# Feed-forward up product as seven block products, with the block sums spread over VectorE and GpSimd

## What is computed

```
h = layer_norm(DN_ALPHA * x + m, ln1_g[i], ln1_b[i])
f = jnp.square(jax.nn.relu(h @ mlp_w1[i])) @ mlp_w2[i]
e = jax.nn.sigmoid(h @ ple_w_gate[i]) * (p[i] @ ple_w_proj[i])
x = layer_norm(DN_ALPHA * h + f + e, ln2_g[i], ln2_b[i])
```

```
mod = jax.nn.silu(c.astype(F32)) @ w_ada + b_ada
```

## Time and profile before

| | us |
|---|---|
| median of 3 runs | 2377.9 |
| lowest and highest | 2377.06, 2378.38 |
| span of the profiled execution | 2375.1 |
| around the span, up to the median | 2.8 |

### The profile page before, as it was taken

How to read it: one execution, slowest core, us unless ns; L and a number is a source line. 1 busy time by engine, 2 the same in 40 slices (tenths; PEclk the granted TensorE clock), 3 DMA queues, 4 the chain that set the end, 5 groups by cost and what they waited for, 6 DMA issues and landing times.

```text
span 2375.1 us, 30964 instructions
## 1 busy us (share of the span) xinstructions
PE 2250.5 (95%) x13454; PEld 1516.2 (64%) x13454; DVE 737.4 (31%) x1301; ACT 411.4 (17%) x845; POOL 523.9 (22%) x451
## 2 busy tenths in 40 slices
PE   9999999999999999999988888899999998888887
PEld 8776676686668899888333333378998863333333
DVE  5533224524216755523100000055753221000001
ACT  3320112620103331211000000033112020000001
POOL 2387622257752045000000000012530000000000
PEclk9999999999999999999999999999999999999999
DMA  7377732358751442349999999953332799999998
GB/s 278 109 309 285 304 133 86 129 193 339 303 217 65 138 143 90 107 168 400 425 428 428 428 428 428 416 212 114 121 136 97 283 409 427 427 428 428 428 427 317
DMA packets 136850, 654.76 MB, mean 276 GB/s; under 512 B 9864, under 2 KB 15112, under 8 KB 108168
## 3 DMA queue, kind: packets, MB, share of 16 engines
q1 hardware_dynamic: 136712, 652.72, 69.0%
HBM read 651.64 MB, written 1.05 MB: 275 GB/s over the span
## 4 chain that ended last, share of the span: by engine, by line
PE 73%; DMA 21%; DVE 3%; ACT 1%; issue 1%; SPq 0%; POOL 0%; DVEq 0%; ACTq 0%
PE bank L798 72%; DMA ring<-in_w_exp_up 11%; DMA PRGT<-in_w_exp_up 5%; DMA PRGT<-in_w_exp_down 3%; DMA PRGT<-in_w_exp_gate 1%; ACT R L3378 1%; PE bank L1428 0%; DVE sm L2174 0%; POOL PRGT L3476 0%; SPq L712 0%; DMA ring<-in_hy_w_in 0%; ACT SQ L3418 0%; PE bank L984 0%; DVE PRGT L2652 0%; DVE PRGT L2168 0%
## 5 line engine op out<-in xcount | busy, mean ns | idle before, releaser
L798 PE MATMUL bank<-hT,ring 128*128 128x256 f32 (+1 forms) x2912 | 607.8, 367 | 0.0
L798 PEld LDWEIGHTS bank<-hT,ring 128*128 128x128 f32 x2912 | 521.5, 190 | 81.5 <-issue 15.3
L798 PE MATMUL bank<-PRGT,R 128*32 128x512 f32 x1120 | 278.7, 612 | 27.8 <-DMA PRGT<-in_w_exp_up 16.7
L798 PE MATMUL bank<-ring,R 128*32 128x512 f32 (+1 forms) x992 | 251.2, 587 | 39.0 <-DMA ring<-in_w_exp_up 23.2
L3590 POOL TENSOR_TENSOR SQ<-xT 128x512 f32<-128x512 f32 x4 | 4.2, 1057 | 1187.9 <-DVE xT L2927 1187.7
L798 PE MATMUL bank<-PRGT,ring 128*128 128x256 f32 (+6 forms) x1328 | 223.0, 359 | 0.4 <-ACT PRGT L3133 0.4
L798 PE MATMUL bank<-PRGT,SQ 128*32 128x512 f32 (+2 forms) x864 | 194.6, 530 | 14.4 <-ACT SQ L3418 12.2
L798 PEld LDWEIGHTS bank<-PRGT,ring 128*128 128x128 f32 (+3 forms) x1328 | 186.4, 175 | 32.0 <-issue 3.0
L798 PEld LDWEIGHTS bank<-PRGT,R 128*32 128x32 f32 x1120 | 75.6, 112 | 191.7 <-issue 191.2
L798 PEld LDWEIGHTS bank<-ring,R 128*32 128x32 f32 (+1 forms) x992 | 69.9, 114 | 168.3 <-issue 168.0
L798 PE MATMUL bank<-ring,SQ 128*32 128x512 f32 (+2 forms) x640 | 167.7, 519 | 8.5 <-ACT SQ L3418 8.3
(11 more groups left out here) (427 smaller groups left out, 2491.7 us busy)
## 6 DMA issues: line engine op xcount, KB each, us to landing
PRGT<-in_w_exp_gate SPq DMA_DIRECT2D x42, 2048.0 KB, 31.9
ring<-in_w_exp_up SPq DMA_DIRECT2D x36, 2048.0 KB, 31.9
ring<-in_mlp_w SPq DMA_DIRECT2D x32, 2048.0 KB, 8.9
PRGT<-in_w_exp_down SPq DMA_DIRECT2D x30, 2048.0 KB, 30.9
PRGT<-in_w_exp_up SPq DMA_DIRECT2D x28, 2048.0 KB, 32.1
PRGT<-in_w_ada SPq DMA_DIRECT2D x32, 1536.0 KB, 12.4
ring<-in_w_exp_down SPq DMA_DIRECT2D x24, 2048.0 KB, 33.6
ring<-in_w_exp_gate SPq DMA_DIRECT2D x22, 2048.0 KB, 32.1
```

The costliest lines, as they stand in the source:

```text
L798: return mm(o, lhsT=lhsT, rhs=rhs, start=first, stop=last, **kw)
```

## The change

The up product of pairs 2 to 15 is also taken as seven block products: the width is split into two halves, the pair's columns into two and the tokens into two, and a block product is four matmuls of 128 columns. All go into the one bank `ff_bank`. Its first 128 columns collect the common corner; ScalarE copies three intermediate states of it (`corner`), and TensorE waits for each copy before it writes the bank again. Behind each of these three points stands one piece of the down product of pair `q - 2`, and the four others follow at the end (`hidden_and_down`); so the down product trails by two pairs, where it trailed by one.

VectorE gets a new order (`feed_forward`): sums of the tokens, once per layer; per pair the column sums of the up weights two pairs ahead (`up_sums`), the row sums that GpSimd had, and three additions that join the corner copies with the rest of the bank (`up_joined`); the `w_ada` sums are spread between them, the first three in the turn of pair 1. The token sums lie in `R`, the column sums in `xT` and `SQ`, one of them in place in the weight tile. GpSimd keeps the sums of the down weights, all 16 pairs in a row. ScalarE's ReLU follows the join, by halves (`squared`). SP's stream is unchanged. To stay within the number of semaphores, some early ones are merged (`c_sig` into `lam_steps`, `gelu_steps` into `conv_done`), and counts that are shared with the dense stage are shifted.

```diff
+UP_SEVEN = tuple(range(2, FF_PAIRS))
...
+        def up_block(l, q, kb, h):
+
+            W = ring[SLOT_AT[f"mlp{l}"][2 * (q % 4 // 2)][0]][:, :].rearrange("p (k n) -> p k n", k=KT)
+            c = (2 * (q % 2) + h) * P
+            return W[:, 4 * kb:4 * kb + 4, c:c + P]
+
...
+        UP_T = [k4(flat(R[:, 2 * r:2 * r + 2, :])) for r in range(4)]
+        UP_S = [[k4(flat(t)) for t in (xT[:, 0:2, :], xT[:, 2:4, :], SQ[:, 4:6, :])],
+                [k4(flat(t)) for t in (xT[:, 4:6, :], xT[:, 6:8, :], SQ[:, 6:8, :])]]
+        UP_CORNER = [small_w[:, 0:3 * P], hsum3[:, 0:3 * P]]
+        UP_REST = [small_w[:, 3 * P:6 * P], flat(stat[:, :, :])[:, 0:3 * P]]
...
                 slots = SLOT_AT[f"mlp{l}"]
                 ready = normed(KT)
 
+                def product(dst, lhs, rhs, first=False):
+                    for k in range(4):
+                        ins = mul(dst, lhs[:, k, :], rhs[:, k, :], first and k == 0, False, skip_group_check=True)
+                    return ins
+
+                def hidden_and_down(q):
+
+                    x, z, y1, y = regions(ff_bank(l))
+                    t1, t2, t3, t4 = UP_T
+                    s1, s2, s4 = UP_S[q % 2]
+                    n = up_at(l, q)
+                    product(x, up_block(l, q, 0, 0), h_block(0, 0), True).then_inc(sems["corner_full"], 1)
+                    down(q - 2, range(0, 1))
+                    pe.wait_ge(sems["corner_read"], 3 * n + 1)
+                    product(z, up_block(l, q, 1, 0), h_block(1, 0))
+                    pe.wait_ge(sems["sums_ready"], n + 1)
+                    product(y, s1, t1)
+                    product(x, s2, t2).then_inc(sems["corner_full"], 1)
+                    down(q - 2, range(1, 2))
+                    pe.wait_ge(sems["corner_read"], 3 * n + 2)
+                    product(y1, s4, h_block(1, 1))
+                    product(x, up_block(l, q, 0, 1), t3).then_inc(sems["corner_full"], 1)
+                    down(q - 2, range(2, 3))
+                    pe.wait_ge(sems["corner_read"], 3 * n + 3)
+                    product(x, up_block(l, q, 1, 1), t4).then_inc(sems["ff_full"], 1)
+                    down(q - 2, range(3, 7))
+
                 def hidden(q):
 
                     i, c, j = q // 4, q % 4 // 2, q % 2
@@ -1099,6 +1150,9 @@
                         pe.wait_ge(bank_read[n % BANKS], filled(n))
                     else:
                         pe.wait_ge(sems["ff_read"], FF_PAIRS * l + q)
+                    if q in UP_SEVEN:
+                        hidden_and_down(q)
+                        return
                     W = slot(s, KT)
                     for h in range(2):
                         for k in range(KT):
@@ -1108,7 +1162,7 @@
                                       k == 0, k == KT - 1)
                     ins.then_inc(sems["ff_full"], 1)
 
-                def down(q):
+                def down(q, part=range(7)):
 
                     if q == 0:
                         for n in range(BANK_AT[f"ple_proj{l}"] + 1, BANK_AT[f"ple_proj{l}"] + 4):
@@ -1116,21 +1170,25 @@
                     i, c = q // 4, q % 4 // 2
                     s, u = slots[2 * c + 1]
                     pe.wait_ge(slot_full[s], loaded(u, i))
-                    pe.wait_ge(sems["ff_act"], FF_PAIRS * l + q + 1)
+                    pe.wait_ge(sems["ff_act"], 2 * (FF_PAIRS * l + q + 1))
+                    pe.wait_ge(sems["wsum_ready"], FF_PAIRS * l + q + 1)
                     pe.wait_ge(sems["asum_ready"], FF_PAIRS * l + q + 1)
                     a11, a12, a21, a22 = ff_blocks(q)
                     b11, t3, b21, b22 = down_blocks(s, q)
                     t1, t2, t4 = WSUM[q % 2]
                     s1, s2, s3, s4 = (ASUM[q % 2][:, r, :] for r in range(4))
-                    for o, lhs, rhs in zip(corners(l), (a11, a12, s4, a22, s1, s2, s3), (b11, b21, b22, t4, t1, t2, t3)):
+                    products = list(zip(corners(l), (a11, a12, s4, a22, s1, s2, s3), (b11, b21, b22, t4, t1, t2, t3)))
+                    for m in part:
+                        o, lhs, rhs = products[m]
                         ins = mul(o[:, :], lhs, rhs, q == 0, q == FF_PAIRS - 1, skip_group_check=True)
-                    ins.then_inc(sems["down_done"], 1)
+                    if m == 6:
+                        ins.then_inc(sems["down_done"], 1)
 
                 hidden(0)
                 proj_half(1)
                 for q in range(1, FF_PAIRS):
                     hidden(q)
-                    down(q - 1)
+                down(FF_PAIRS - 2)
                 down(FF_PAIRS - 1)
...
-            def ada(l):
-
-                a0 = 16 * l
-
-                def half(k, h):
-                    dve.wait_ge(sems[f"ada_loaded{h}"], k * 16 + (8 * a0 + 16))
-                    total = ADA_SUM[:, h * ADA_N:(h + 1) * ADA_N]
-                    if isinstance(k, int):
-                        v.tensor_scalar(total, ADA[h], sm[:, CS:CS + 1], None, ALU.mult).then_inc(sems["ada_summed"], 1)
-                    else:
-
-                        dve.wait_ge(sems["ada_summed"], k * 2 + (a0 + h - 1))
-                        v.scalar_tensor_tensor(total, ADA[h], sm[:, bass.ds(k, 1)], total, ALU.mult, ALU.add).then_inc(
-                            sems["ada_summed"], 1)
-                half(0, 0)
-                half(0, 1)
-                with nc.vector.Fori(1, KT) as k:
-                    half(k, 0)
-                    half(k, 1)
+            def ada(l, m):
+
+                k, h = divmod(m, 2)
+                dve.wait_ge(sems[f"ada_loaded{h}"], 16 * (KT * l + k + 1))
+                total = ADA_SUM[:, h * ADA_N:(h + 1) * ADA_N]
+                if k == 0:
+                    v.tensor_scalar(total, ADA[h], sm[:, CS:CS + 1], None, ALU.mult).then_inc(sems["ada_summed"], 1)
+                else:
+                    dve.wait_ge(sems["ada_summed"], 16 * l + m - 1)
+                    v.scalar_tensor_tensor(total, ADA[h], sm[:, CS + k:CS + k + 1], total, ALU.mult, ALU.add).then_inc(
+                        sems["ada_summed"], 1)
+
+            def stepped(ins):
+                ins.then_inc(sems["vec_chain"], 1)
+                dve.wait_ge(sems["vec_chain"], L.up())
+
+            def token_sums():
+
+                t1, t2, t3, t4 = UP_T
+                b11, b12, b21, b22 = h_block(0, 0), h_block(0, 1), h_block(1, 0), h_block(1, 1)
+                stepped(v.tensor_tensor(t1, b12, b11, ALU.subtract))
+                v.tensor_tensor(t2, b22, t1, ALU.subtract)
+                stepped(v.tensor_tensor(t3, b22, b12, ALU.subtract))
+                v.tensor_tensor(t4, b21, t2, ALU.subtract)
+
+            def up_sums(l, q):
+
+                s, u = SLOT_AT[f"mlp{l}"][2 * (q % 4 // 2)]
+                dve.wait_ge(slot_full[s], loaded(u, q // 4))
+                a11, a12, a21, a22 = (up_block(l, q, kb, h) for h in range(2) for kb in range(2))
+                s1, s2, s4 = UP_S[q % 2]
+                v.tensor_tensor(s1, a21, a22, ALU.add)
+                stepped(v.tensor_tensor(a21, a11, a21, ALU.subtract))
+                stepped(v.tensor_tensor(s2, s1, a11, ALU.subtract))
+                v.tensor_tensor(s4, a12, s2, ALU.subtract).then_inc(sems["sums_ready"], 1)
+
+            def row_sums(l, q):
+
+                if q >= 2:
+                    dve.wait_ge(sems["down_done"], FF_PAIRS * l + q - 1)
+                dve.wait_ge(sems["ff_act"], 2 * (FF_PAIRS * l + q + 1))
+                a11, a12, a21, a22 = ff_blocks(q)
+                s1, s2, s3, s4 = (ASUM[q % 2][:, r, :] for r in range(4))
+                v.tensor_tensor(s1, a21, a22, ALU.add)
+                stepped(v.tensor_tensor(s3, a11, a21, ALU.subtract))
+                stepped(v.tensor_tensor(s2, s1, a11, ALU.subtract))
+                v.tensor_tensor(s4, a12, s2, ALU.subtract).then_inc(sems["asum_ready"], 1)
+
+            def up_joined(l, q):
+
+                c, rest, f0 = UP_CORNER[q % 2], UP_REST[q % 2], 2 * (q % 4)
+                dve.wait_ge(sems["ff_read"], FF_PAIRS * l + q + 1)
+                stepped(v.tensor_tensor(FF[:, f0, :], c[:, 0:2 * P], rest[:, 0:2 * P], ALU.add))
+                v.tensor_tensor(FF[:, f0 + 1, P:S], c[:, 2 * P:3 * P], rest[:, 2 * P:3 * P], ALU.add)
+                v.tensor_tensor(FF[:, f0, P:S], FF[:, f0, P:S], rest[:, 2 * P:3 * P], ALU.add).then_inc(sems["ff_joined"], 1)
+
+            def feed_forward(l):
+
+                token_sums()
+                up_sums(l, 2)
+                for q in range(FF_PAIRS):
+                    if q in UP_SEVEN:
+                        up_joined(l, q)
+                    if q == 1:
+                        ada(l, 0)
+                        ada(l, 1)
+                    if 1 <= q < FF_PAIRS - 1:
+                        ada(l, q + 1)
+                    if q and q + 2 in UP_SEVEN:
+                        up_sums(l, q + 2)
+                    row_sums(l, q)
 
             def ffn_and_ple(l):
-                ada(l)
+                feed_forward(l)
...
```

(91 more changed lines are left out.)

6 lines of the change are left out of this document (3 added, 3 removed).

## The result

The changed kernel takes 2386.85 us (median of 5 runs, 2386.54 to 2387.42), the kernel before, run beside it on the same chip, 2377.06 (5 runs). The ratio is 1.0041, with a 95% interval of 1.0029 to 1.0053: slower by 9.8 us. The prediction was 2392 in a range of 2380 to 2405, slower. The profiled span went from 2375.1 to 2385.6 us.

What follows compares the result with a forecast made beforehand. TensorE was taken to bound the feed-forward stages, busy throughout at full clock. Terms -17.9 + 1.7 + 22.8 + 5.6 + 2 = +14.2 us on the 2375.1 span, plus 2.8 to the median, gave 2392 us, range 2380 to 2405.

Steps and rivals of the forecast that it cites:

- Passes: TensorE, pairs 2 to 15: 56 passes of 128 columns replace 32 of 256, saving 17.9 us over two layers.
- Bank waits: TensorE's waits for the three corner copies per pair: each hidden behind a 0.86 us down product, so 0.
- Order: Pair 2's hidden product directly follows pair 1's and waits for its bank read: 0.85 us a layer, +1.7.
- VectorE's queue at the start: TensorE in pair 3 waits for pair 1's row sums, queued behind the DMA-paced third w_ada sum: +22.8 us, both layers.
- the lower end of 15.3: Startup wait with the port free of GpSimd: 7.2 us in layer 0 and 8.1 in layer 1.
- Slow clock: TensorE's clock falls after the long idle stretch at the start: 2.8 us a layer, +5.6.
- Steady state: Pairs 3 to 13: GpSimd's sums blocking VectorE make its turn exceed TensorE's pair; 0 to 13 us, taken as +2.
- full turn of 12.87: VectorE's time per pair if each of GpSimd's four operations blocks it for 1.13 us, against TensorE's 12.28.
- the startup wait: TensorE's wait in pair 3 of each layer for VectorE's row sums of pair 1: 11.3 and 11.5 us.

Runs made afterwards that it cites:

- version 2: Against the changed kernel, every VectorE sum TensorE awaits stands ahead of possibly late w_ada sums, and SP issues fewer w_ada loads ahead of the weights; 2360.61 us.
- the filler: Against the changed kernel, 23 calls of products whose result is not used stand ahead of pair 3's first product in each layer; 2385.10 us.
- experiment 7: Against the kernel with awaited sums first and fewer w_ada loads ahead of the weights, two more column sums a pair from pair 4 on; 2385.38 us.

## Why the prediction was right, term by term

- **Passes, -17.9.** Right: a pair takes 12.27 us, 12.28 predicted, and version 2 shows the gain in the time.
- **Bank waits, 0.** Right, and in the 24 pairs tried the cover is worth 45 us by the timeline (0.63 a copy, between the 0.48 and 0.68 of the bounds) and 48 by the medians.
- **Order, +1.7.** The wait is 0.78 a layer: +1.6.
- **VectorE's queue at the start, +22.8.** The step that decides was right in mechanism, place (pair 3's first down product) and releaser; measured 10.77 + 10.14 = +20.9. In layer 0 it is 10.77 for 11.3: three column sums met a GpSimd operation, as forecast, but paid 1.06 + 1.05 + 0.94 = 3.05 more than 0.69, where 3.4 was taken. In layer 1 it is 10.14 for 11.5, of two errors that partly cancel: all four paid, 4.0, but the third w_ada sum ended 15.6 us after pair 2 began (526.63 to 542.22), where the earlier trace rows made it 17.3 with the bank read between. Without GpSimd 15.2 is left, beside the lower end of 15.3; that is luck in part, since the layers are 7.86 and 7.36, and the forecast had 7.2 and 8.1. The Trainium skill (SBUF — State Buffer, section "SBUF: two separate sides") has the loser of the port pair stand still for the other's whole instruction. This trace agrees: a column sum takes 0.69 alone and 1.75 against a GpSimd sum (1.27 alone), and GpSimd's own takes 4.36 behind a w_ada sum.
- **Slow clock, +5.6.** 25.86 - 12.27 - 10.77 = 2.82 and 25.17 - 12.27 - 10.14 = 2.76: +5.6, and the filler shows that it is the clock, for at least 5.1 of it.
- **Steady state, +2.** Measured 0: no wait after pair 3 in either layer. GpSimd did lengthen column sums throughout (1.46 us in the mean for the first of them, line 2303), but it is done early enough in each turn. The forecast's full turn of 12.87 was too long: by experiment 7 it is 11.97, under the pair, so all four of GpSimd's sums could block VectorE in every pair and the turn would still be shorter than the pair.

Sum: -17.9 + 1.6 + 20.9 + 5.6 = +10.2, against +10.5 of the span and +9.8 of the medians. The +14.2 was high by terms that were mis-sized, 1.9 in the startup wait and 2 in the steady state. No mechanism was missing; that the startup wait came so near owes something to the errors in layer 1 that cancel.

## What to carry to other kernels

When work moves onto an engine with spare time, write down its new queue in order and ask of each instruction what it may have to wait for: here 973 us busy of 2386 was no problem, while one DMA-paced sum ahead of an awaited one cost more than the whole change gained. Put what another engine waits for ahead of what waits for a transfer. Then do the same for the queue that issues the transfers: reordering one of two queues that release each other can close a ring, and cost 114 us where the matching order costs nothing. And do not count all idle time as room: with VectorE idle for 1.9 us a pair, 1.54 us of added work cost 1.05.
